# Two-block network on one core: free weight places join the ring earlier, three modulation pieces move into the routing, attention scores take four banks

## What is computed

```python
for layer in range(2):
    m = modulation(silu(c), w_mod[layer], b_mod[layer])     # 1024 -> 6*1024, the same for the context
    u = h * (1 + m[1]) + m[0]
    y = attention_and_pooling(u, u_ctx) if layer == 0 else short_conv(u)
    h = layer_norm(ALPHA * h + m[2] * y)
    h = layer_norm(ALPHA * h + m[5] * experts(h * (1 + m[4]) + m[3]))

# attention: 8 query heads, 2 key heads of 64; 512 queries against 256 + 512 keys
s = q @ k.T / 8;  p = softmax(s);  o = p @ v
# pooling branch: four groups of 128 features, windowed mean minus own value, times w_pool_grp[g]
# experts: 16 experts, each takes the 64 tokens with the highest affinity:
aff = softmax(u @ w_router);  gate, idx = top_k(aff, 64)
ye = (silu(u[idx] @ w_gate) * (u[idx] @ w_up)) @ w_down * gate      # 3 x 4 MB of weights per expert
```

## Time and profile before

| | |
|---|---|
| median of three timed runs | 2973.08 us |
| the profiled execution | 2988.05 us |
| its span, first to last instruction | 2986.3 us |
| PE busy | 2777.0 us (93%) |
| DVE busy | 1170.2 us (39%) |
| ACT busy | 806.2 us (27%) |
| POOL busy | 127.4 us (4%) |
| mean granted clock of PE | 0.946 |
| moved by DMA | 601.11 MB, mean 201 GB/s |

### The profile page before, as it was taken

One profiled execution on the slowest core, in us unless ns is written; L12 is line 12 of the kernel. 1 busy time (PEld: TensorE's weight loads), 2 busy tenths in 40 slices (PEclk: granted clock), 3 DMA queues, 4 the chain that ended last, 5 costly groups with the idle time before them and its releaser, 6 DMA issues.

```text
span 2986.3 us, 32682 instructions
## 1 busy us (share of the span) xinstructions
PE 2777.0 (93%) x13724; PEld 1811.1 (61%) x13724; DVE 1170.2 (39%) x1704; ACT 806.2 (27%) x1240; POOL 127.4 (4%) x124
## 2 busy tenths in 40 slices
PE   6998899998899979999988998999999999999998
PEld 4555534343368544443336777878778756787886
DVE  4464512111164341121126554323334588633333
ACT  2353311010032121110014334222232465532222
POOL 1210100000000110000001010000010000000000
PEclk9999899999989979999999999999999899999999
DMA  8860699999932079999991212232241300132220
GB/s 296 315 229 16 259 401 426 427 425 421 425 117 97 16 300 385 426 428 428 427 406 64 83 57 85 85 113 71 89 137 43 79 1 1 57 120 75 98 89 36
DMA packets 125651, 601.11 MB, mean 201 GB/s; under 512 B 7440, under 2 KB 12880, under 8 KB 100672
## 3 DMA queue, kind: packets, MB, share of 16 engines
q1 hardware_dynamic: 120128, 584.27, 49.3%
q0 software_dynamic: 5376, 14.75, 1.6%
HBM read 596.90 MB, written 2.10 MB: 201 GB/s over the span
## 4 chain that ended last, share of the span: by engine, by line
PE 76%; DVE 10%; DMA 9%; ACT 4%; issue 1%; DVEq 0%; POOL 0%; SPq 0%; ACTq 0%
PE psum L295 73%; DMA weight_ring<-in_w_exp_down 5%; DVE scratch L245 3%; ACT scratch L283 3%; PE psum L310 3%; DMA scratch<-in_w_exp_down 2%; DVE scratch L3636 1%; DVE scratch L278 1%; DVE scratch L258 1%; DMA weight_ring<-in_w_mix_in 1%; DVE h L245 1%; DVE scratch L1408 0%; DMA weight_ring<-in_w_exp_up 0%; DMA scratch<-in_w_exp_up 0%; DVE scratch L1819 0%
## 5 line engine op out<-in xcount | busy, mean ns | idle before, releaser
L295 PE MATMUL psum<-scratch,scratch 128*128 128x512 f32 (+13 forms) x9384 | 1900.7, 401 | 57.7 <-DVE scratch L245 20.6
L295 PEld LDWEIGHTS psum<-scratch,scratch 128*128 128x128 f32 (+3 forms) x9384 | 1391.5, 182 | 530.6 <-issue 216.8
L295 PE MATMUL psum<-weight_ring,scratch 128*64 128x512 f32 (+2 forms) x2752 | 673.8, 632 | 56.5 <-DMA weight_ring<-in_w_exp_down 23.7
L295 PEld LDWEIGHTS psum<-weight_ring,scratch 128*64 128x64 f32 (+2 forms) x2752 | 216.2, 143 | 467.2 <-issue 393.5
L283 ACT ACTIVATE scratch<-psum 128x512 f32<-128x512 f32 (+4 forms) x330 | 192.9, 585 | 1001.3 <-PE psum L310 545.4
L245 DVE TENSOR_TENSOR scratch<-weight_ring,scratch 128x2048 fp32r<-128x2048 f32 (+2 forms) x110 | 241.9, 2199 | 494.3 <-ACT scratch L283 492.9
L283 ACT ACTIVATE scratch<-weight_ring 128x2048 fp32r<-128x2048 f32 (+2 forms) x122 | 218.7, 1793 | 581.3 <-PE psum L295 558.3
L245 DVE TENSOR_TENSOR scratch<-scratch,psum 128x512 f32<-128x512 f32 x92 | 63.3, 688 | 530.2 <-PE psum L295 528.8
L310 PE MATMUL psum<-consts,scratch 128*128 128x128 f32 x1116 | 173.3, 297 | 58.0 <-DVE scratch L245 41.2
L245 DVE TENSOR_TENSOR scratch<-scratch,scratch 128x512 fp32r<-128x512 f32 (+12 forms) x355 | 199.4, 562 | 58.7 <-ACT scratch L283 43.0
L310 PEld LDWEIGHTS psum<-consts,scratch 128*128 128x128 f32 x1116 | 135.4, 164 | 125.5 <-issue 49.5
(11 more groups left out here) (106 smaller groups left out, 722.9 us busy)
## 6 DMA issues: line engine op xcount, KB each, us to landing
weight_ring<-in_w_exp_gate SPq DMA_DIRECT2D x44, 2048.0 KB, 15.0
weight_ring<-in_w_exp_down SPq DMA_DIRECT2D x44, 2048.0 KB, 13.2
weight_ring<-in_w_exp_up SPq DMA_DIRECT2D x43, 2048.0 KB, 15.5
weight_ring<-in_ffn_w SPq DMA_DIRECT2D x28, 2048.0 KB, 7.7
weight_ring<-in_w_mod SPq DMA_DIRECT2D x24, 2048.0 KB, 9.0
scratch<-in_w_exp_up SPq DMA_DIRECT2D x21, 2048.0 KB, 15.7
scratch<-in_w_exp_gate SPq DMA_DIRECT2D x20, 2048.0 KB, 15.1
scratch<-in_w_exp_down SPq DMA_DIRECT2D x20, 2048.0 KB, 12.4
```

What stands on the lines that cost most here:

```text
L295: ins = T.eng.matmul(out, lhsT, rhs, start=start, stop=stop)
```

## The change

- `widen` gets a position. In layer 0 the two more places come in during attention, before modulation piece 2, and at the head of the list; in layer 1 when the convolution has ended, behind the first place of the list.
- `lend` puts the lent places at the head of the list, and is called after two expert pieces in layer 0 and after five in layer 1, instead of before the first.
- Modulation pieces 9, 10 and 11 are all multiplied in the routing; `first_pe` is gone.
- The scores take four banks: each head has two of its own, and the wait between the halves is gone. `VALUES` moves to bank 4, `TURNED` has banks 5, 6 and 7.

```diff
--- before.py
+++ after.py
@@ -155,17 +155,17 @@
     def slot(self, i):
         return (self.base + self.more + self.lent)[i]
 
-    def widen(self, Y, stage):
+    def widen(self, Y, stage, at):
 
         for name in ("pe", "dve", "act"):
             Y.wait_ge(*self.k.at("end", stage, name))
-        self.slots += [len(self.base) + i for i in range(len(self.more))]
+        self.slots[at:at] = [len(self.base) + i for i in range(len(self.more))]
 
     def lend(self, Y, stage):
 
         for name in ("pe", "dve", "act", "pool"):
             Y.wait_ge(*self.k.at("end", stage, name))
-        self.slots += [len(self.base) + len(self.more) + i for i in range(len(self.lent))]
+        self.slots[0:0] = [len(self.base) + len(self.more) + i for i in range(len(self.lent))]
 
     def drop(self, i):
         self.slots.remove(i)
@@ -648,18 +648,14 @@
         self.steps = self.HALVES - 3
 
     def rest_sync(self, Y):
-        self.load_half(Y, self.steps)
-        self.k.ring.widen(Y, AttnInputs.KEY)
-        for j in range(self.steps + 1, self.HALVES):
+        for j in range(self.steps, self.HALVES):
             self.load_half(Y, j)
-
-    def first_pe(self, T):
-        self.products(T, self.steps, (0, 7))
 
     def rest_pe(self, T):
         a, b, c = range(self.steps, self.HALVES)
+        self.products(T, a, self.BANKS)
+        self.products(T, b, self.BANKS)
         self.sums(T, a, self.BANKS)
-        self.products(T, b, self.BANKS)
         self.products(T, c, self.BANKS)
         self.sums(T, b, self.BANKS)
         self.sums(T, c, self.BANKS)
@@ -909,8 +905,6 @@
                 self.next.logits_pe(T, t - 2)
             if t:
                 self.next.turn_pe(T, t - 1)
-        if self.rest:
-            self.rest.first_pe(T)
         self.next.turn_pe(T, NT - 1)
         T.end(self.key)
         self.next.logits_pe(T, NT - 2)
@@ -1239,7 +1233,7 @@
 
 
     KEY = "attention"
-    SCORES, VALUES, TURNED = (0, 3), (3, 4), (4, 8)
+    SCORES, VALUES, TURNED = (0, 4), (4, 5), (5, 8)
     BUFS = 3
 
     def __init__(self, k, m, inputs, filler):
@@ -1257,6 +1251,8 @@
 
     def sync(self, Y):
         for j in range(self.filler.steps):
+            if j == 2:
+                self.k.ring.widen(Y, AttnInputs.KEY, 0)
             self.filler.step_sync(Y, j)
 
     def pool(self, G):
@@ -1309,17 +1305,15 @@
     def scores(self, T, n):
         k = self.k
         g, t = self.steps[n]
-        run = k.psum.take(T, ("scores", n), self.SCORES, 3)
-
-        for i, bank, at, n0, n1 in ((0, 0, 0, 0, 512), (1, 1, 256, 0, 256), (1, 2, 0, 256, self.N), (0, 1, 0, 512, self.N)):
-            q = slice(64 * i, 64 * i + 64)
-            if bank == 1 and i == 0:
-                T.wait_ge(*k.at("scores apart", n))
-            names = {(1, 1): [("scores apart", n)], (2, 1): [("scores right", n)], (1, 0): [("full", "scores", n)]}.get((bank, i), [])
-            mm(T, run[:, bank, at:at + n1 - n0], self.x.qT[q, g, t * P:(t + 1) * P], self.x.kT[q, n0:n1], True, True, *names)
+        run = k.psum.take(T, ("scores", n), self.SCORES, 4)
+        for b, (n0, n1) in enumerate(((0, 512), (512, self.N))):
+            for i in range(2):
+                q = slice(64 * i, 64 * i + 64)
+                mm(T, run[:, 2 * i + b, 0:n1 - n0], self.x.qT[q, g, t * P:(t + 1) * P], self.x.kT[q, n0:n1], True, True,
+                   *([("full", "scores", n)] if b and i else []))
 
     def score_view(self, n):
-        return self.k.psum.of(("scores", n)).rearrange("p b n -> p (b n)").rearrange("p (i n) -> p i n", i=2)
+        return self.k.psum.of(("scores", n)).rearrange("p (i b) n -> p i (b n)", i=2)[:, :, 0:self.N]
 
     def transposes(self, T, n, i):
         k = self.k
@@ -1719,9 +1713,10 @@
 
     def sync(self, Y):
         k, d = self.k, self.k.dram
-        if not self.rest:
-            k.ring.widen(Y, self.before)
-        k.ring.lend(Y, self.before)
+        if self.layer:
+            k.ring.widen(Y, ShortConv.KEY, 1)
+
+        own = 5 if self.layer else 2
         for what, e in self.order():
 
 
@@ -1730,6 +1725,9 @@
                 k.ring.drop(len(k.ring.base) + given)
             for name in {"up": ("w_exp_gate", "w_exp_up"), "down": ("w_exp_down",)}.get(what, ()):
                 for i in range(2):
+                    if own == 0:
+                        k.ring.lend(Y, self.before)
+                    own -= 1
                     k.ring.load(Y, (self.key, name, e, i), long_rows(d[name][self.layer, e], i))
         k.ring.narrow()
 
```

## The result

The kernel after took 2996.57 us in the median of four runs (2993.87 to 2997.67), beside four of the kernel before at 2973.16. The ratio, with its 95% interval, is 1.0057 [1.0034, 1.0079], which on 2973.08 is 2990.0 us. Both intervals lie wholly above 1.002: the change is slower. The forecast of 2987.6 lies between the two; the first median by itself is 0.6 us beyond the upper end of the range.

A forecast was written before the change was run, and what follows sets the result against it. The prediction took the weight DMA stream to bound the experts and a chain of engines to bound attention. Attention +4.2, its clock +8.4, layer 0 +1.9 and layer 1 0 gave +14.5 on 2973.1: 2987.6 us, range 2974 to 2996.

The forecast's parts named there:

- scores: Attention: four banks remove the wait between halves, 0.34 us a step, 16 times, plus 0.3 in step 1: gain 5.7 us.
- waits of C, net of the old ones: Attention steps 7, 9, 11, 13: second head's first four transposes wait for the pooled product's evacuation; loss 9.9 us.
- clock behind them: Attention: after each of the four 3.6 us idles PE's clock falls to 0.5, costing +8.4 us, bounds 0 and 12.
- attention, whole: Attention: +4.2 us from shorter scores and new waits, and +8.4 from the clock behind the waits.
- mixer end and routing: Moved modulation: net +0.6 us at the mixer's end, -1.7 in the routing from a shorter PE idle.
- order of places, layer 0: Layer 0's experts: pieces 16 to 18 wait for 11 to 13 instead of 10 to 12; +3.0 us.
- experts, layer 1: Layer 1's experts: a stream pause swallows any head start, later dependences unchanged; 0 us, bounds -1.7 and +1.
- Rival (a): Attention: the waits come but the clock stays up; +6.1 us in all, 2979.2 us; chance 0.2.
- Rival (b): Clock falls deeper: four waits cost 3.0 us each, no recovery in the routing; +21.8, 2994.9 us; chance 0.15.
- Rival (c): Experts: seven early weight pieces shorten the DMA-bound stretch by 34 us; 2953 us; decided at piece 8; chance 0.07.
- Rival (d): Attention: the pooled product frees its bank without holding the transposes, so four banks pay; -3.8, 2969.3 us; chance 0.08.
- it may even help: Routing: moved modulation shortens PE's idle, keeping the clock up for the row groups; -1.7 us, bounds 0 and -3.4.

The follow-up runs named there:

- `ring_mod_only`: The kernel after with the scores back in three banks, leaving only the weight places and moved modulation: 2979.57 us, ratio 1.0000 to the kernel before.
- `lend_fifth`: The kernel after with the pooled product evacuated ahead of the exponentials and layer 0's places lent after five pieces, not two: 2971.65 us, ratio 0.9975 to before.
- `pout_early`: The kernel after with ACT's evacuation of the pooled product moved ahead of both exponentials of its step: 2969.75 us, ratio 0.9971 to the kernel before.
- `banks_pout_early`: The kernel before with four score banks and the pooled product evacuated ahead of the exponentials, weight places and modulation unchanged: 2970.02 us, ratio 0.9971 to before.
- `stall_filled`: The kernel after with the second transposes made seven times in steps 7, 9, 11 and 13, filling PE's wait: 2985.69 us, ratio 1.0023 to before.
- `base_again`: The kernel before, unchanged, timed and profiled once more: 2981.59 us, ratio 1.0013 to the kernel before.
- `three_banks_pout_early`: The kernel before with only the pooled product's evacuation moved ahead of both exponentials: 2972.18 us, ratio 0.998 to the kernel before.

## Why the prediction came out as it did

| term | predicted | measured | from |
|---|---|---|---|
| scores | -5.7 | -4.1 | 118.6 and 114.5 us of attention |
| waits of C, net of the old ones | +9.9 | +8.0 | 12.9 less 4.9, of which some 1.2 is clock |
| clock behind them | +8.4 | +7.3 to +8.5 | 126.3 and 133.6 or 134.8 |
| attention, whole | +12.6 | +10.2 to +11.4 | 123.4 and 133.6 or 134.8 |
| mixer end and routing | -1.1 | +0.1 to +1.3 | 104.4 and 104.5 or 105.7 |
| order of places, layer 0 | +3.0 | +2.3, +3.2 | `ring_mod_only`, `lend_fifth` |
| fall of the clock in layer 0's experts | not foreseen | +3.2 | piece 15 at 44.6, not 41.4 |
| experts, layer 1 | 0 | -3.0 to +1.0 | table of stages; -3.0 where the clock did not fall |

(The first three measured terms add to 11.2 to 12.4; the 1 us that is missing from the whole is the difference between the attention of `pout_early` and of `banks_pout_early`, 113.5 and 114.5, which have the same banks.)

**The main mechanism was right.** The waits are in the four steps named, 3.61 us each where 3.6 was said, released by ACT, and the clock is at its lower level behind each, in all for 20.5 us in the first profile of after and 17.1 in the second. The forecast took half of 4 x 4.2, 16.8. (One of its nine readings is off: behind the 4.36 us of the earlier trace rows the clock stayed at 0.50 for 7.5 us and not 6.1 at most, which makes the mean 4.9 and not 4.6.) Rival (a), that the clock stays up, falls: `stall_filled` shows 7.3 to 8.5 us of it. This agrees with the Trainium skill (TensorE: Matmul & The Clock Gate, HAM oscillation), where a loop that waits in each pass, there for a DMA, starts each pass throttled; the price comes from the runs. Rival (b), a clock that stays low through the routing, falls too: 26.8 to 27.6 us against 27.2. Rival (c), the early places, falls at the point named: in layer 0 piece 8 goes out 3.7 us behind expert 0's start in eleven profiles and 3.8 in that of before, whether the seventh piece has landed by then (0.3 us behind the start in the kernel after) or not (8.2 in the unchanged one). Rival (d) falls with the four idle stretches.

**Scores, mis-sized.** A step of scores is 0.33 us shorter at the same clock, against the 0.34 forecast, so the price was right and the multiplier wrong: "they lie on the path 16 times" holds for the last twelve steps, and the first three gain nothing. The prediction set the rule of the Trainium skill (TensorEngine Tiling (Array Packing), PSUM Bottleneck), taken at its strictest (all 5.7 us lost to the evacuation; the page itself says that the copy may become the bottleneck), against the chain, and kept the chain. The 4.1 us bear that out for the late steps, where scores and evacuation follow one another. In the first three PE waits for ACT, whose exponentials read the scores out of PSUM, and there the page's caution holds.

**Waits, net.** The sum counted the two old waits at 1.7 to 1.8 us, and that is what they are. Taking them away gives 4.9, not 3.5, because in the unchanged kernel's second profile the clock fell behind the second, as above. An estimate from the steps (0.83, and 0.39 of the 2.09) puts this at 1.2 us. Without it the new waits cost +9.2 net, near the +9.9 forecast, and the clock, less what it already cost before, 6.1 to 7.3 against 8.4. What the sum had left out is that an old wait can have its fall of the clock too; in the profile that it started from it had none.

**Routing.** The step that said "it may even help" failed. PE's timeline of the kernel after:

```profile
361.34 0.61 PE L310 MATMUL psum<-consts,scratch 16*128 16x16 f32 x4 [2.91 <-DVE scratch L245]
362.64 6.14 PE L295 MATMUL psum<-scratch,scratch 128*128 128x512 f32 x16 [0.69 <-issue]
```

The logits, ahead of these rows, take 7.01 us, as layer 1's did, and as forecast. The idle ahead of the ranks is 2.91 instead of 4.36, but the clock falls all the same and the row groups take 6.14, not 3.4. In its second profile the idle is 1.71 and they take 5.50, in `ring_mod_only` 1.81 and 5.51. The 6.77 of the earlier trace rows lay wholly inside a fall of the clock; in `base_again` the unchanged kernel takes 5.76. Routing and mixer together came out +0.1 to +1.3 against `base_again`, whose 104.4 is the shortest with the modulation of before; the seven profiles with the moved pieces take 104.0 to 105.9, the four with the old order and full clock 104.4 to 105.9. So the move is worth nothing that these profiles can tell. The -1.7 was half of a chance that did not come in any profile of this case: the groups take 5.50 us or more in all.

**Layer 0's experts.** The order of the places cost what the walk through the list said. On top came a fall of the clock that stands in the profile of before only in layer 1 (granted clock 0.50 from 1133.7 to 1140.5, not quoted among the rows above). PE's timeline of the kernel after and, behind it, of the unchanged kernel, the transposes behind the gates, some 37 us behind the start of expert 0:

```profile
410.19 1.95 PE L310 MATMUL psum<-consts,scratch 128*128 128x128 f32 x8
```

```profile
398.33 1.18 PE L310 MATMUL psum<-consts,scratch 128*128 128x128 f32 x8
```

Eight transposes in 1.95 instead of 1.18 us, and no idle row ahead of them in either. In the kernel after the fall begins at 408.4, while the two-column matmuls of the gates run (405.9 to 410.2). Neither the four banks nor the weight places are needed for it: it is in the profile of `three_banks_pout_early`, which has the banks, the weight places and the modulation of before. In nine of the twelve profiles of this case layer 0 has it, and the three without (before, `base_again`, `ring_mod_only`) are just those whose attention is that of before. So it may go with any change in attention, for instance by the times at which later work falls. Why it comes is open; no run here shows it.

**The sum.** Attention was forecast 1.2 to 2.4 us too high, routing and mixer 1.2 to 2.4 too low, layer 0's experts 2.4 to 3.0 too low, and layer 1's between 3.0 too high and 1.0 too low. The five stages add to +19.7 us in the first profile of after and to +12.7 in the second; the forecast was +14.5. So 2987.6 lies between the two results (2990.0 and 2984.1) in part by luck: a fall of the clock that it did not have made good for what it put too high in attention. The spans of these profiles differ from the unchanged kernel's by 12.8 and 4.5 us only, because the rest behind layer 1's experts, the same in all kernels, took 1429.6 and 1429.7 us in them and 1435.8 in `base_again`.

**What would have been faster.** The four banks are worth having once the evacuation of "p out" stands ahead of the exponentials: 0.9971 [0.9957, 0.9986], some 2964.5 us on 2973.08, below both kernels. The early evacuation by itself, with three banks, gives 0.998 [0.9966, 0.9994]: the two can't be told apart by the whole time, only by the 4.1 us of attention.

## What to carry to other kernels

When a bank is taken from a shared ring, write out the takes in order and look at which of them now waits for which evacuation, and where that evacuation stands in its engine's own queue: a copy of 0.7 us behind two exponentials cost 12.9 us in four steps, and moving it ahead of them turned a loss of 0.4 to 0.6% into a gain of 0.3%. Price an idle stretch of PE with the slower work behind it: here 3.6 us of idle cost about another 2. An early start of loads is worth nothing where the stream next waits for a place, and there the order of the list of places decides, here by 2 to 3 us of the stage. And take two profiles of the unchanged kernel before pricing a term of a few microseconds: here they differed in where the clock fell.

## What the hardware showed that was not expected

- The granted clock fell to 0.50 for 6.8 us without an idle stretch of PE just ahead of it (the last in the kernel after, 0.84 us, lay 21 us back), in the midst of 32 matmuls of two columns (1.95 us for the eight transposes behind them instead of 1.18). In layer 1 one profile of the kernel after has this fall and the other has not. What brings it is not shown.
- Two profiles of one unchanged kernel had granted clocks of 0.91 and 0.96 over the same 500 us (0.949 and 1.00 outside the falls), and differ by 7 us (2988.05 and 2981.04). Against the first the profile of after is 5.8 us longer, against the second 12.8. Their rows by stretch, of before and of the unchanged kernel's second profile, are much alike in the work (the second gets 27 more matmuls done) and not in the clock:

```profile
1000.00:1500.00 500.00, 464.27 (x1980) 205.71 (x1978) 122.66 (x196) 72.52 (x115) 17.95 (x7) 0.91 0.86 363
```

```profile
1000.00:1500.00 500.00, 451.20 (x2007) 203.06 (x2007) 121.53 (x193) 72.58 (x115) 17.23 (x7) 0.96 0.88 374
```

- Around short idles of PE the clock sometimes fell and sometimes not: in the routing it fell by an idle of 2.91 us in the kernel after and behind idles of 1.81 and 0.69 us in `ring_mod_only`; in attention of the unchanged kernel it fell behind 1.70 us and not behind 1.79.
- The part of the program behind layer 1's experts is the same in every kernel here. It took 1428.1 to 1436.3 us in the twelve profiles, with 61 to 81 us of it at a granted clock of 0.50.
